# Rotary positions in three attention blocks: rows exchanged by small DMAs and VectorE instead of by products with an exchange matrix

## The reference, cut to what matters

```
x1 = t[..., :half]            # half = 8
x2 = t[..., half:ROPE_DIM]    # ROPE_DIM = 16
rot = concat([x1 * cos - x2 * sin, x2 * cos + x1 * sin])
return concat([rot, t[..., ROPE_DIM:]])
```

## Time and profile before

| | |
|---|---|
| median of 3 runs | 2201.39 us (2201.37 to 2201.58) |
| the profiled execution | 2201.32 us, of which its span 2199.5 us |
| TensorE granted clock | 0.999 (the level of 2.4 GHz) |
| busy: PE, PEld, DVE, ACT, POOL | 99%, 78%, 53%, 28%, 68% |
| DMA moved | 195.83 MB, 28.5% of 16 engines on SyncE's queue |

### The profile page before, as it was taken

The page is one execution under the profiler, slowest core; times in us unless marked ns, Lnnn a source line. Parts: engine busy times, 40 slices in busy tenths (PEclk is TensorE's granted clock), DMA queues, the critical chain, the costliest instruction groups (busy, mean ns, idle before and its releaser), DMA issues.

```text
span 2199.5 us, 29816 instructions
## 1 busy us (share of the span) xinstructions
PE 2175.3 (99%) x10944; PEld 1724.8 (78%) x10945; DVE 1175.8 (53%) x1960; ACT 608.3 (28%) x1441; POOL 1486.8 (68%) x677
## 2 busy tenths in 40 slices
PE   9999999999999999999999999999999999999998
PEld 6876788888877767778888888777677788888887
DVE  8769667774355285547650243462765477411423
ACT  5238322221011165531220121111555412200210
POOL 7660787778876614449887888766334397887884
PEclk9999999999999999999999999999999999999999
DMA  5320233333334311113333333333111132333332
GB/s 194 115 77 1 68 96 96 97 97 103 105 99 129 118 30 51 56 58 98 95 97 98 97 101 97 96 115 115 58 47 50 58 96 86 106 96 96 96 96 77
DMA packets 56073, 195.83 MB, mean 89 GB/s; under 512 B 7441, under 2 KB 9489, under 8 KB 55697
## 3 DMA queue, kind: packets, MB, share of 16 engines
q1 hardware_dynamic: 54224, 189.42, 28.5%
q10 hardware_dynamic: 1728, 4.70, 0.6%
HBM read 191.87 MB, written 2.10 MB: 88 GB/s over the span
## 4 chain that ended last, share of the span: by engine, by line
PE 91%; DVE 5%; issue 1%; ACT 1%; DMA 0%; POOL 0%; SPq 0%; DVEq 0%; POOLq 0%
PE bank L545 26%; PE bank L547 26%; PE bank L546 26%; PE bank L733 3%; PE bank L743 3%; PE bank L780 1%; PE bank L762 1%; DVE t L1475 1%; PE bank L783 1%; DVE prow L1600 1%; PE bank L621 1%; DVE bank L1589 1%; PE bank L690 1%; ACT prow L1193 1%; DMA w_raw<-wstream 0%
## 5 line engine op out<-in xcount | busy, mean ns | idle before, releaser
L473 POOL TENSOR_TENSOR w_hi<-w_raw,zero 128x1024 fp32r<-128x1024 f32 x334 | 646.2, 1935 | 661.1 <-PE bank L547 643.5
L476 POOL TENSOR_TENSOR w_lo<-w_raw,w_hi 128x1024 fp32r<-128x1024 f32 x334 | 840.0, 2515 | 26.2
L545 PE MATMUL bank<-hn_hi,w_hi 128*128 128x512 f32 x1616 | 643.2, 398 | 3.9 <-POOL w_lo L476 2.0
L547 PE MATMUL bank<-hn_hi,w_lo 128*128 128x512 f32 x1616 | 630.5, 390 | 0.0
L546 PE MATMUL bank<-hn_lo,w_hi 128*128 128x512 f32 x1616 | 629.4, 389 | 0.0
L545 PEld LDWEIGHTS bank<-hn_hi,w_hi 128*128 128x128 f32 x1616 | 303.5, 188 | 72.4 <-issue 6.0
L547 PEld LDWEIGHTS bank<-hn_hi,w_lo 128*128 128x128 f32 x1616 | 303.3, 188 | 65.0
L546 PEld LDWEIGHTS bank<-hn_lo,w_hi 128*128 128x128 f32 x1616 | 303.8, 188 | 60.9 <-issue 1.4
L545 PE MATMUL bank<-hid_hi,w_hi 128*128 128x512 f32 x672 | 261.4, 389 | 0.0
L546 PE MATMUL bank<-hid_lo,w_hi 128*128 128x512 f32 x672 | 261.4, 389 | 0.0
L547 PE MATMUL bank<-hid_hi,w_lo 128*128 128x512 f32 x672 | 261.4, 389 | 0.0
(11 more groups left out here) (322 smaller groups left out, 2701.7 us busy)
## 6 DMA issues: line engine op xcount, KB each, us to landing
w_raw<-wstream SPq DMA_DIRECT2D x352, 512.0 KB, 3.6
x<-xT SPq DMA_DIRECT2D x4, 512.0 KB, 7.5
out<-yout SPq DMA_DIRECT2D x12, 128.0 KB, 1.9
mem_x<-memT SPq DMA_DIRECT2D x1, 1024.0 KB, 12.2
lnc<-lncount ACTq DMA_DIRECT2D x1, 1024.0 KB, 6.1
cs<-trig ACTq DMA_DIRECT2D x2, 512.0 KB, 4.1
par<-params ACTq DMA_DIRECT2D x1, 696.0 KB, 5.4
bc<-bconst ACTq DMA_DIRECT2D x1, 664.0 KB, 7.3
```

The source lines that it names most:

```text
L473: nc.gpsimd.tensor_tensor(w_hi[:, slot, :], w_raw[:, slot, :], zeros, ALU.add).then_inc(w_rounded, 1)
L476: nc.gpsimd.tensor_tensor(w_lo[:, slot, :], w_raw[:, slot, :], w_hi[:, slot, :].bitcast(f32), ALU.subtract).then_inc(w_split, 1)
L545: nc.tensor.matmul(ps[bank][:, 0:cols_], wh, a_h, start=c == 0, stop=False)
L547: mm = nc.tensor.matmul(ps[bank][:, 0:cols_], wl, a_h, start=False, stop=c == chunks - 1)
```

## The change

The product with `rot` goes for q and k tiles in all three blocks. In its place VectorE multiplies the tile by a signed sine into an SBUF buffer (`tmp`, in the layers `rope_v`) and by the cosine back into its own bank. ScalarE then issues four DMAs for the tile, each of 8 partitions x 2 KB (16 KB) from that buffer into `rope_w`, from rows 8 to 15 to rows 0 to 7 and back, for both heads. All four count on one semaphore (two in turn), 64 for a tile. VectorE adds `rope_w` to the bank and reports the bank as free. The rows of `rope_w` that no DMA writes are zeroed once before each block. The sine table gets its sign (in the first block by a second `Sin` of 32 columns and by which part a table DMA reads).

The core of the diff:

```
-                    if t in ROPE:
-                        pe.wait_ge(qk_raw, QK[t] + 1)
-                        rotate(ROPE[t], tmp[:, ROPE[t] % 2, :])
...
-                    if kind in ("qr", "kr"):
-                        pe.wait_ge(rot_rounded, l + 1)
-                        pe.wait_ge(rope_split, 6 * l + idx_of_rope(t) + 1)
-                        rotate_split(roped_n, roped_n % 2)
...
+        SWAPPED = ((0, 8), (8, 0), (64, 72), (72, 64))
+            def move_rows(n, src):
+
+                act.wait_ge(rope_in, n + 1)
+                for to, at_ in SWAPPED:
+                    act.dma_start(rope_w[to:to + 8, n % 2, :], src[at_:at_ + 8, :]).then_inc(rope_moved[n % 2], 16)
...
-            A(trig[:, :, :], angle[:, 0:2, :], ACT.Sin).then_inc(trig_packed, 1)
+            A(trig[:, 0:2, :], angle[:, 0:2, :], ACT.Sin)
+            A(trig[:, 2, :], angle[:, 0, :], ACT.Sin, scale=-1.0).then_inc(trig_packed, 1)
...
-                            A(tmp[:, ROPE[t] % 2, :], ps[bank][:, :], ACT.Identity,
-                              scale=neg_g[:, 0:1] if kind == "q" else pcol("k_g")).then_inc(qk_raw, 1)
...
+                        if t in ROPE:
+                            move_rows(ROPE[t], tmp[:, ROPE[t] % 2, :])
                         act.wait_ge(qk_var, e + 1)
...
-                            A(rope_hi[:, rn % 2, :], src[:, :], ACT.Copy,
-                              scale=-0.125 if kind == "qr" else 1.0).then_inc(rope_in, 1)
+                            n = len(ROPE) + 6 * l + idx_of_rope(t)
+                            move_rows(n, rope_v[:, n % 2, :])
...
+            V.memset(rope_w[:, :, :], 0.0)
             V.memset(conv_in[:, :, 0:HALO], 0.0)
...
+                        dve.wait_ge(qk_sq, QK[t] + 1)
+                        V.scalar_tensor_tensor(out=tmp[:, ROPE[t] % 2, :], in0=ps[bank][:, :], scalar=g_, in1=sin1[:, :],
+                                               op0=ALU.mult, op1=ALU.mult).then_inc(rope_in, 1)
+                        link(V.scalar_tensor_tensor(out=ps[bank][:, :], in0=ps[bank][:, :], scalar=g_, in1=cos1[:, :],
+                                                    op0=ALU.mult, op1=ALU.mult))
...
                 for _ in range(IN1_TAPS.get(i, 0)):
                     conv_tap()
+                if 0 <= i - 1 < len(IN1) and IN1[i - 1] in ROPE:
+                    n, bank = ROPE[IN1[i - 1]], tiles[IN1[i - 1]][4]
+                    dve.wait_ge(rope_moved[n % 2], 64 * (n // 2 + 1))
+                    V.tensor_tensor((t1, ri)[n % 2][:, :], ps[bank][:, :], rope_w[:, n % 2, :], ALU.add).then_inc(dve_took, 1)
...
-                V.tensor_copy(rot_r[:, :], rot).then_inc(rot_rounded, 1)
+                V.memset(rope_w[:, :, :], 0.0)
...
+                        for m, out_ in ((1, rope_v[:, n % 2, :]), (0, ps[bank][:, :])):
+                            ins = V.scalar_tensor_tensor(out=out_, in0=ps[bank][:, :],
+                                                         scalar=-0.125 if kind == "qr" else 1.0, in1=cs2[:, m, :],
+                                                         op0=ALU.mult, op1=ALU.mult)
...
+                        dve.wait_ge(rope_moved[n % 2], 64 * (n // 2 + 1))
+                        V.tensor_tensor((qb if kind == "qr" else ksw)[:, idx, :], ps[bank][:, :], rope_w[:, n % 2, :],
+                                        ALU.add).then_inc(dve_took, 1)
```

More of the change, by code:

```diff
@@ L215, in build @@
         csc_kept, trig_scaled = sem("csc_kept"), sem("trig_scaled")
-        rope_split, rot_rounded = sem("rope_split"), sem("rot_rounded")
+        rope_moved = [sem(f"rope_moved{i}") for i in range(2)]
         rs_kept, rs_applied, rope_in, gated = sem("rs_kept"), sem("rs_applied"), sem("rope_in"), sem("gated")
@@ L267, in build @@
         ROPE = {t: n for n, t in enumerate(t for t in IN1 if tiles[t][0] in ("q", "k"))}
+        RAW = {t: n for n, t in enumerate(t for t in IN1 if tiles[t][0] in ("qm", "km"))}
+        SWAPPED = ((0, 8), (8, 0), (64, 72), (72, 64))
         TURNED = {t: n for n, t in enumerate(t for t in IN1 if tiles[t][0] in ("v", "vm"))}
@@ L441, in _ @@
                 for row in (0, 8, 64, 72):
+                    part = 2 if n == 0 and row in (8, 72) else n
                     sp.dma_start(full[row:row + 8, :].rearrange("f (a j) -> f a j", a=16),
-                                 trig[:, n, :]).then_inc(trig_ready, 16)
+                                 trig[:, part, :]).then_inc(trig_ready, 16)
             for n, (b0, b1) in enumerate(RUNS):
@@ L1387, in _ @@
                         kind, idx, _, _, bank = tiles[t][:5]
-                        if kind in ("qr", "kr"):
-                            act.wait_ge(blocks_done, filled(t))
-                        elif kind not in ("cp", "w1"):
+                        if kind not in ("cp", "w1", "qr", "kr"):
                             act.wait_ge(rs_applied, SCALED[t])
@@ L1841, in _ @@
                 for i in range(len(jobs) + 2):
-                    if 0 <= i - 2 < len(jobs) and tiles[jobs[i - 2]][0] in ("qr", "kr"):
-                        t = jobs[i - 2]
-                        kind, idx, _, _, bank = tiles[t][:5]
-                        dve.wait_ge(fg_parts, l + 1)
+                    if i < len(jobs) and tiles[jobs[i]][0] in ("qr", "kr"):
+                        kind, _, _, _, bank = tiles[jobs[i]][:5]
+                        n = len(ROPE) + 6 * l + idx_of_rope(jobs[i])
@@ L1846, in _ @@
                         dve.wait_ge(trig_scaled, 2 * (l + 1))
-                        dve.wait_ge(roped, roped_n - len(ROPE))
-                        dve.wait_ge(rotated, roped_n + 1)
-                        V.scalar_tensor_tensor(out=t1[:, :], in0=ps[bank][:, :], scalar=-0.125 if kind == "qr" else 1.0,
-                                               in1=cs2[:, 0, :], op0=ALU.mult, op1=ALU.mult).then_inc(dve_took, 1)
-                        link(V.tensor_tensor(ps[5][:, :], ps[5][:, :], cs2[:, 1, :], ALU.mult))
@@ new lines, in _ @@
+                    if 0 <= i - 1 < len(jobs) and tiles[jobs[i - 1]][0] in ("qr", "kr"):
+                        kind, idx, _, _, bank = tiles[jobs[i - 1]][:5]
+                        n = len(ROPE) + 6 * l + idx_of_rope(jobs[i - 1])
+                        dve.wait_ge(rope_moved[n % 2], 64 * (n // 2 + 1))
+                        V.tensor_tensor((qb if kind == "qr" else ksw)[:, idx, :], ps[bank][:, :], rope_w[:, n % 2, :],
+                                        ALU.add).then_inc(dve_took, 1)
@@ L2123, in _constants @@
     ang = (i[None, :].astype(f) * inv).astype(f)
-    trig2 = np.stack([np.cos(ang), np.sin(ang)], axis=1).astype(f)
+    sign = np.where(p % 64 // 8 == 1, f(-1), f(1))
+    trig2 = np.stack([np.cos(ang), sign[:, None] * np.sin(ang)], axis=1).astype(f)
     return fconst, bconst, np.ascontiguousarray(lnc), np.ascontiguousarray(trig2)
```

88 lines of the change are left out of this document (24 added, 64 removed).

## The result

The changed kernel takes 2205.19 us (median of 20 runs, 2202.55 to 2205.94), the one before on the same chips 2201.64 us (2201.2 to 2203.81): a ratio of 1.0014 with a 95% interval of 1.0007 to 1.0020. It is 3.5 us slower, little but clear of zero, where I forecast 0.9 us faster. The profiled execution took 2205.94 us, its span is 2204.2.

The account below looks back on a forecast made before the run. TensorE was taken to bound the kernel, level with VectorE in the first block. First-block stage +3.5, memset +1.0 and layers -5.4 gave -0.9 us, so 2200.5 us, with 2193.5 to 2207.5 for 8 in 10.

Parts of the forecast that it names:

- the mechanism named for the first block: First block: ScalarE issues four DMAs before the square root VectorE waits for, so VectorE's cycle sets the pace.
- the forecast's own range: Whole kernel: the no-change case, X from 1.7 to 3.2 with the landing hidden, 2197 to 2205.8 us, chance 0.52.
- X: First block: ScalarE's time for the four DMA issues of a tile, taken as 2.3 us, ends 1.3 and 2.8.
- The table DMAs' row: Profile row of the only 8-partition DMAs, four in 2.77 us, 0.69 each; it would make X 2.8.
- The formula: First block: a VectorE cycle of q, k and km tiles takes 16.53 + 2X; the stage changes by 6X - 10.3.
- -1.8: First block, first q, k pair: VectorE has slack, so the gain of 2 exchange products (1.8 us) comes in full.
- the landing hidden behind 3.5 us: First block, q pass: VectorE reaches the DMA wait 3.5 us after the last issue ends; landing taken to cost 0.
- The memset: First block: zeroing `rope_w` on VectorE takes 0.96 us on the path, +1.0 us, bounds 0 and 1.0.
- The layers: Hybrid layers: 6 tiles x 2 layers x 0.45 us of TensorE products go, no landing waits, -5.4 us.
- A (issues of 1.6 us): Faster rival, first block: four issues take 1.6 us or less, sum -5.1 or better (2196 us); chance 0.32.
- B (a late landing): Slower rival, first block: DMAs land late, +4.7 us or, at 5.5 us, +11.1 (2212.5); chance 0.16, including X well over 3.
- the wider range: Whole kernel: the range for 8 in 10, from 2193.5 (X near 1.1) to 2207.5 us (X near 3.3 or landing 4.9).

Follow-up runs that it names:

- e7_16_rows: The changed kernel with each of the first block's four row moves over 16 partitions (32 KB) in place of 8 (16 KB); 2203.17 us, ratio 1.0005.
- e5_two_moves: The changed kernel with two of the four row moves left out in the first block; 2196.75 us, ratio 0.9976 to the kernel before.
- e3_sqrt_first: The changed kernel with ScalarE's square root ahead of the four DMA issues in the first block; 2198.3 us, ratio 0.9984 to the kernel before.
- e4_products_kept: The changed kernel with two unread TensorE products where each exchange product of the first block stood; 2205.31 us, ratio 1.0017 to the kernel before.
- the layers alone: Row moves by DMA only in the hybrid layers, first block as in the kernel before; 2196.97 us, ratio 0.9977; repeated: 2197.17 us, 0.9978.

## Why the prediction was wrong

The direction was wrong, by the size of terms; the mechanism named for the first block was the right one. The measured 2205.19 us lie inside the forecast's own range of 2197 to 2205.8, but at its upper end, and in the profiled execution 3.3 us of them come from the clock, for which the forecast had no term.

- **X, the step that failed.** I took 2.3 us "by the middle of these two" rows; it is 2.65. At 6 us per us of X that is +2.1 us, and by itself turns -0.9 into +1.2. The table DMAs' row (0.69 for one, 8 partitions) was close to the truth, and the plain 0.45 was not a reason to go half way. The 0.69 is itself drawn up by one issue of 0.81 us: the four cos table DMAs behind them, of the same form, are at 0.61 each (the L442 row under `e7_16_rows`). The third value, 50 ns, which the Trainium skill ("DMA: Bandwidth & Descriptors", section "Anatomy of one DMA") gives for the dispatch, stands there for DMAs issued by GpSimd, and these are ScalarE's. `e5_two_moves` shows the dose, `e3_sqrt_first` the place.
- **The formula.** With 2.65 a cycle should be 21.8 us; measured 21.61 and, with the low clock in it, 22.89; with the clock up (`e4_products_kept`) 21.56 and 21.72. The last pair cost more than the formula has: from its q pass to the mark 162.60 - 121.30 = 41.3 us against 154.81 - 117.82 = 37.0 before, +4.3 for 2.5, of which the clock is 0.4 and the longer X of the last pass another 0.4. Up to the second q pass the kernel was faster than forecast, by 2.3 us (76.80 against 79.08) where -1.8 and the memset's +1.0 were written. In all, the stage should be +5.6; measured +7.6 (the +7.8 of the mark less the 0.2 of the memset), of which 1.6 us are the clock's. That leaves +6.0. That it ends only 0.4 from the formula is luck: the error of the last pair and that of the start have opposite signs. The idle time, its place and who ends it, the wait of TensorE and the landing hidden behind 3.5 us (2.0 to 3.4 in `e3_sqrt_first`) were as written, and so was the estimate of 0.10 for the semaphore (the issues begin at 77.58, 0.78 behind the start of a sine product of 0.67, so it is 0.11). The forecast had no term for VectorE's late loop letting TensorE wait so long that its clock fell.
- **The clock in the attention**: 1.7 us in the profiled execution, nothing in the forecast. It is an event that the last section comes back to.
- **The memset**: +1.0 forecast, +0.2 measured. The stalled `mn_lo` operations behind it became shorter (4.28 us for four before, in the row below, 1.67 after), so it took up time in which VectorE would have been held anyway. The memset is not the whole delay either: the scaling behind it began 2.8 us later than before, and 1.7 of them are the held L1691.

```profile
32.46 4.28 DVE L1515 SCALAR_TENSOR_TENSOR mn_lo<-mem_x,par,mn_hi 128x256 fp32r<-128x256 f32 x4
```

- **The layers**: -5.4 forecast, -4.9 measured alone (-2.4 for each layer in the marks). TensorE has no wait for a landing, as forecast; VectorE has six (22.5 us in all, 5.1 at the longest), in time in which it has nothing else to do. Right.
- **Rivals.** A (issues of 1.6 us) and B (a late landing) both did not occur. `e5_two_moves` is in effect rival A, with X at 1.33: it measured 2196.75 us, and the forecast's sum for 1.3 was 2194.5. The upper end of the wider range was drawn a little wrong: X of 3.3 gives 2206.5 by the forecast's own sum, not 2207.5, which needs the landing of 4.9 us or X of 3.5.

Together: -0.9 + 2.1 (X) + 0.4 (formula) - 0.8 (memset) + 0.5 (layers) + 1.6 + 1.7 (clock) = +4.6, against +4.7 in the spans.

## What to carry to other kernels

A DMA from SBUF to SBUF issued by an engine that also computes costs that engine 0.6 us here, and what counts is who waits for the instruction behind the issues: put the issues behind the result that another engine needs, which alone turned +3.5 us into -3.5. Where the price of a new instruction lies between two rows of which only one has its form, the sum must go by that row, above all where it carries a factor of six. When a change makes the bounding engine wait, look for what the wait does afterwards (the granted clock of the next window), and when an operation's operands move to SBUF, look at GpSimd's operations beside it.

## What the runs showed of the hardware that I had not expected

- **The clock can fall after short waits.** Behind waits of 1.1 to 1.6 us, beside products of 2 or 128 columns, TensorE was granted the lower level for 8 to 13 matmuls, three times in the first block and once in an attention. The profile of the kernel before never shows it. The wait alone does not decide it: `e4_products_kept` has the same wait of 1.13 us in the attention, without a fall. In an attention it comes or stays away with one and the same kernel: the layers alone had a span of 2195.0 us in one profile, with the clock at 1.00 throughout, and of 2196.7 in the other, with this window in layer 2's attention:

```profile
1555.00:1565.00 10.00, 8.69 (x55) 5.21 (x55) 8.01 (x33) 6.71 (x23) 0.00 (x0) 0.83 0.17 52
```

  So some 1.7 us of any difference between two single profiles can be this event, and of the +4.7 us above 1.7 are. The kernel before may have it too: 24 of its 89 executions beside the kernels of this document lie at 2202.9 to 2203.8 us and the others at 2201.2 to 2202.2, a gap of about this size, though none of the 24 is among the profiles. Whether the change makes it more frequent was not measured.
- **A busier TensorE gave the clock and no time.** With the granted clock at 0.999 over the run in place of 0.995, `e4_products_kept` was as slow as the changed kernel.
- **The price of an issue** from SBUF to SBUF is 0.63 us on ScalarE for 16 KB and 0.61 for 32 KB, and 0.61 on SyncE for the tables; a store of 128 KB from SBUF takes ScalarE 0.34.
- **GpSimd holds VectorE.** A sum of 0.69 us stretched to 2.3 where both inputs lay in SBUF and a GpSimd operation was running; with one input in PSUM it did not. The L1691 operation, with one input in SBUF, took 1.88 us in place of 0.18 when it began 0.05 us after a `w_hi` operation (31.12 to 33.01) and not ahead of it. The memset that cost 0.2 instead of 0.9 us stood ahead of operations whose inputs all lie in SBUF; that these were held in the same way was not tried.
